# Rewriting the recurrent mixer of a two-block network: chunks of 64 tokens, one instruction block, key projection first

## The reference, cut to what matters

```python
def step(S, inp):                      # one token, state S per head: 64 x 64
    sa = einsum('bhvk,bhk->bhv', S, -kk_t)
    S = S * w_t + sa[..., None] * kka_t + v_t[..., None] * k_t
    y = einsum('bhvk,bhk->bhv', S, r_t)

xx = shift(h) - h;  xs = h + xx * mu           # six mixes: r, k, v, w, a, g
r, k, v = xs[:3] @ w_rkv                       # three 1024 x 1024 projections
decay   = exp(-exp(-softplus(-(w0 + tanh(xw @ w_la) @ w_lb)) - 0.5))
a = sigmoid(a0 + (xa @ a_la) @ a_lb);  g = sigmoid(xg @ g_la) @ g_lb
kk = normalise_per_head(k * k_k);  k = k * (1 + (a - 1) * k_a)
y = scan(step, r, decay, k, v, kk, kk * a)     # over 256 tokens
y = (group_norm(y) + bonus(r, k, r_k, v)) * g;  out = y @ w_o
```

## Time and profile before

| what | value |
|---|---|
| median of 3 runs | 2202.36 us (2195.92 to 2205.94) |
| the profiled execution, its time | 2182.94 us |
| its span | 2181.2 us |
| PE busy | 1899.2 us, 87% of the span |
| DVE busy | 830.6 us, 38% |
| ACT, POOL busy | 508.2 us, 138.0 us |
| mean granted PE clock | 0.926 |
| DMA traffic | 554.34 MB, 254 GB/s over the span |

### The profile page before, as it was taken

How to read it: one execution, slowest core, us unless ns; L and a number is a source line. 1 busy time by engine, 2 the same in 40 slices (tenths; PEclk the granted TensorE clock), 3 DMA queues, 4 the chain that set the end, 5 groups by cost and what they waited for, 6 DMA issues and landing times. The chain is left out here.

```text
span 2181.2 us, 28996 instructions
## 1 busy us (share of the span) xinstructions
PE 1899.2 (87%) x11494; PEld 1193.7 (55%) x11494; DVE 830.6 (38%) x1543; ACT 508.2 (23%) x807; POOL 138.0 (6%) x127
## 2 busy tenths in 40 slices
PE   6888599989989888898888789889988966898997
PEld 5675333333333333333333379779977656867996
DVE  7852511111111111111111266565543565446554
ACT  4421211101111110111111055345421141004442
POOL 3301210000000000000000000000000060200000
PEclk9968699999999999999999989999999986579998
DMA  7020699999999999999997275284425002108440
GB/s 271 34 107 1 257 404 428 428 428 429 428 428 429 428 429 428 429 428 429 428 428 323 101 295 188 78 308 155 154 74 204 0 20 66 52 1 308 154 154 30
DMA packets 99120, 554.34 MB, mean 254 GB/s; under 512 B 17473, under 2 KB 20418, under 8 KB 73618
## 3 DMA queue, kind: packets, MB, share of 16 engines
q1 hardware_dynamic: 99058, 553.49, 62.4%
HBM read 551.37 MB, written 2.10 MB: 254 GB/s over the span
## 5 line engine op out<-in xcount | busy, mean ns | idle before, releaser
L1009 PE MATMUL banks<-ring,xsT 128*64 128x512 f32 x2048 | 458.7, 598 | 41.9 <-DMA ring<-in_w_up 40.9
L1009 PEld LDWEIGHTS banks<-ring,xsT 128*64 128x64 f32 x2048 | 143.2, 137 | 351.3 <-issue 266.0
L1108 DVE TENSOR_SCALAR glu<-banks 128x512 f32<-128x512 f32 x32 | 22.1, 692 | 663.8 <-PE banks L1016 663.8
L1045 PE MATMUL banks<-ring,hT 128*64 128x512 f32 x1024 | 230.2, 603 | 22.0 <-ACT hT L1064 22.0
L1045 PEld LDWEIGHTS banks<-ring,hT 128*64 128x64 f32 x1024 | 71.5, 138 | 158.6 <-issue 130.5
L1546 PE MATMUL banks<-f_xT_hi,f_w_hi 128*128 128x256 f32 x512 | 146.8, 287 | 7.2 <-ACTq L1590 7.2
L1546 PE MATMUL banks<-f_xT_lo,f_w_hi 128*128 128x256 f32 x512 | 146.6, 286 | 0.0
L1546 PE MATMUL banks<-f_xT_hi,f_w_lo 128*128 128x256 f32 x512 | 146.6, 286 | 0.0
L1060 ACT ACTIVATE sig<-glu 128x512 f32<-128x512 f32 x32 | 20.1, 630 | 478.4 <-DVE glu L1108 478.4
L1546 PEld LDWEIGHTS banks<-f_xT_hi,f_w_hi 128*128 128x128 f32 x512 | 100.1, 195 | 9.4 <-DVE f_w_lo L1625 7.6
L1546 PEld LDWEIGHTS banks<-f_xT_lo,f_w_hi 128*128 128x128 f32 x512 | 100.1, 195 | 1.8
(11 more groups left out here) (383 smaller groups left out, 2992.6 us busy)
## 6 DMA issues: line engine op xcount, KB each, us to landing
ring<-in_w_up SPq DMA_DIRECT2D x128, 2048.0 KB, 24.7
ring<-in_w_down SPq DMA_DIRECT2D x64, 2048.0 KB, 20.3
ring<-in_ffn_w SPq DMA_DIRECT2D x32, 2048.0 KB, 7.8
ring<-in_sgu_in SPq DMA_DIRECT2D x8, 2048.0 KB, 7.6
m_raw<-in_w_in SPq DMA_DIRECT2D x7, 2048.0 KB, 10.3
ring<-in_w_rkv SPq DMA_DIRECT2D x6, 2048.0 KB, 20.4
ring<-in_sgu_out SPq DMA_DIRECT2D x4, 2048.0 KB, 7.6
ring<-in_w_out SPq DMA_DIRECT2D x1, 4096.0 KB, 16.4
```

Source lines behind the costliest of these rows:

```text
L1009: ins = nc.tensor.matmul(c.banks[CAP * h:CAP * (h + 1), bank, :], xsT[:, k, :], up_slot[k // 2][:, o:o + BANK], start=k == 0, stop=False)
L1045: ins = nc.tensor.matmul(c.banks[CAP * h:CAP * (h + 1), DOWN, :], hT[:, at:at + CAP], down_slot[half][:, o:o + BANK], start=k == 0, stop=k ...
L1108: v.tensor_scalar(glu[:, :], c.banks[:, GLU, :], LIMIT, None, ALU.min).then_inc(glu_ready, 1)
```

## The change

The stage becomes one instruction block with chunks of 64 tokens (four chunks, two for each 128 tokens), while the systems that are solved stay 32 x 32 (SUB = 32). What it does, by engine:

- PE starts with the k projection's first bank, then the low-rank products with the other k banks behind them, the sum of kk squared, the first bank of r, the spread of the inverse root, the second bank of r, A·B, the last two banks of r, the v projection, then the other grams, transposes, bonus and G_AK·v. A·B and all grams are made only for the 64 x 64 diagonal blocks, in products with 64 rows and 64 columns of the array.
- The value weights are loaded into the memory of the key weights once these are read.
- The two late r banks and the product with kT are taken by DVE inside the solve (`query`).
- The inverse of a 64-token chunk is put together from its two 32 x 32 inverses and the block between them (`own`, `cross`, `add_cross`), applied at once to A and to G_AK·v; P is then transposed.
- The walk has four chunks, of which the first has no incoming state. The output's products are made for each chunk (64 rows, 64 columns).
- The group norm's square moves to ACT, one POOL product (a times the inverse decay) is new, and `head_rk` folds r_k into the bonus selector.

Core of the diff:

```diff
-CH = 32
+CH = 64
...
-        w_rkv_sb = [unit(4 * i, 4).rearrange("p (k n) -> p k n", k=KC) for i in range(3)]
+        w_k, w_r = (unit(i, 4).rearrange("p (k n) -> p k n", k=KC) for i in (0, 4))
+        w_v = w_k
...
+                sp.wait_ge(k_done, 4)
+                for half in range(2):
+                    load_half(w_v, 2, half, v_in)
+                sp.wait_ge(ab_taken, 4)
+                for j in range(P // SUB):
+                    s, t = slice(SUB * j, SUB * (j + 1)), slice(SUB * (j % 2), SUB * (j % 2 + 1))
+                    sp.dma_start(dram_a[j].rearrange("n s t -> s n t"),
+                                 ab[s, :, :, t].rearrange("s c h t -> s (c h) t")).then_inc(a_out, 16)
...
+                for r in range(2):
+                    pe.wait_ge(chained, 2 * r + 2)
+                    for tc in range(TC):
+                        for p in range(4 * r, 4 * r + 4):
+                            for j in range(J):
+                                for par in range(2):
+                                    ins = nc.tensor.matmul(c.banks[rows_of(j), BANKS_AB[2 * r + par], o:o + CH],
+                                                           bT[part(par), p, t], ar[part(par), p, 0, t], start=True,
+                                                           stop=True)
+                    ins.then_inc(ab_done, 1)
+                pe.wait_ge(r_in[1], 16)
+                to_features(w_r, MIX_R, BANKS_R[2], 2, r_done)
+                to_features(w_r, MIX_R, BANKS_R[3], 3, r_done)
...
+                def own(m):
...
+                    for i in range(4):
+                        for j in range(J):
+                            ins = nc.tensor.matmul(c.banks[rows_of(j), m % 4, i * P:(i + 1) * P],
+                                                   inv[rows_of(j), tc, 4 * hq + i, :], right[rows_of(j), tc, 4 * hq + i, :],
+                                                   start=i == 0, stop=False, skip_group_check=True)
+                def cross(m):
...
+                            ins = nc.tensor.matmul(c.banks[late(j), 4 + m % 4, i * P:(i + 1) * P],
+                                                   ab[early(j), tc, h, SUB:CH], pu[early(j), :, tc, at_head(h)],
+                                                   start=True, stop=True)
+                def add_cross(m):
...
+                            ins = nc.tensor.matmul(c.banks[late(j), m % 4, i * P:(i + 1) * P],
+                                                   inv[late(j), tc, 4 * hq + i, SUB:CH], crossed[late(j), m % 4, i, :],
+                                                   start=False, stop=True, skip_group_check=True)
...
+                for tc in range(TC):
+                    for m in range(4 * tc, 4 * tc + 4):
+                        own(m)
+                    for m in range(4 * tc, 4 * tc + 4):
+                        cross(m)
+                    for m in range(4 * tc, 4 * tc + 4):
+                        add_cross(m)
...
+                state_from_values(0)
+                state_from_sa(0)
+                pe.wait_ge(pt_taken, 4)
+                y_from_values(0)
+                y_from_values(1)
+                y_from_sa(0)
+                sa_from_state(1)
+                state_from_values(1)
+                state_from_sa(1)
+                y_from_sa(1).then_inc(y_inner, 1)
+                pe.wait_ge(y_inner, 1)
+                y_from_state(1).then_inc(y_done, 1)
+                y_from_values(2)
+                y_from_values(3)
+                sa_from_state(2)
+                state_from_values(2)
+                state_from_sa(2)
+                y_from_sa(2)
+                sa_from_state(3)
...
+                y_from_sa(3).then_inc(y_inner, 1)
+                pe.wait_ge(y_inner, 2)
+                y_from_state(2)
+                y_from_state(3).then_inc(y_done, 1)
...
+                for t in range(1, SUB):
...
+                    if t == 2:
+                        query(2)
+                    if t == 8:
+                        query(3)
+                        dve.wait_ge(q_ready, 4)
+                        vec.tensor_tensor(prod, ar[:, :, 1, :], kT, ALU.mult).then_inc(prod_ready, 1)
```

More of the change, by code:

```diff
@@ new lines, in second_rank @@
+                def second_rank(lo, bank, b):
+                    for i in range(2):
+                        f = 2 * b + i
+                        ins = nc.tensor.matmul(c.banks[:, bank, i * T:(i + 1) * T],
+                                               wa_lb[lo:lo + LORA, f * P:(f + 1) * P],
+                                               hid[lo:lo + LORA, 0, :], start=True, stop=True)
+                    ins.then_inc(lb_done, 1)
+                pe.wait_ge(lora_in, 64)
+                pe.wait_ge(mixed, 1)
@@ new lines, in _ @@
+                low_rank(w_la, MIX_W, c.banks[0:LORA, 4, 0:T]).then_inc(la_done, 1)
+                pe.wait_ge(mixed, 2)
+                low_rank(a_la, MIX_A, c.banks[LORA:P, 5, 0:T]).then_inc(la_done, 1)
+                pe.wait_ge(mixed, 3)
+                pe.wait_ge(k_in[0], 16)
+                to_features(w_k, MIX_K, BANKS_K[0], 0, k_done)
+                pe.wait_ge(hid_w, 1)
+                for b in range(4):
+                    second_rank(0, BANKS_W_LB[b], b)
+                pe.wait_ge(mixed, 4)
@@ new lines, in _ @@
+                pe.wait_ge(gate_in, 32)
+                low_rank(g_la, MIX_G, c.banks[:, 4, 0:T]).then_inc(g_la_done, 1)
+                pe.wait_ge(hid_a, 1)
+                for b in range(4):
+                    if b >= 2:
+                        pe.wait_ge(sig_taken, b - 1)
+                    second_rank(LORA, BANKS_A_LB[b], b)
+                pe.wait_ge(sig_taken, 3)
+                to_features(w_k, MIX_K, BANKS_K[1], 1, k_done)
+                pe.wait_ge(k_in[1], 16)
+                pe.wait_ge(sig_taken, 4)
@@ L1863, in _ @@
                 ins.then_inc(bonus_done, 1)
[L1865 to L1875 removed]
+                n += 1
+                pe.wait_ge(bonus_taken, 1)
@@ new lines, in y_from_state @@
+                def y_from_state(n):
+                    tc, j = divmod(n, J)
+                    for h in range(RH):
+                        ins = nc.tensor.matmul(
+                            c.banks[rows_of(j), Y_B[2 * tc + h % 2], (h // 2) * HD:(h // 2 + 1) * HD],
+                            ar[part(h), h // 2, 1, n * CH:(n + 1) * CH],
+                            states[part(h), n, (h // 2) * HD:(h // 2 + 1) * HD], start=False, stop=True,
+                            skip_group_check=True)
+                    return ins
@@ L1877, in _ @@
+                for tc in range(TC):
+                    project(tc)
             @block.scalar
@@ new lines, in _ @@
+                act.wait_ge(g_la_done, 1)
+                nc.scalar.activation(hid[:, 1, :], c.banks[:, 4, 0:T], ACT.Sigmoid).then_inc(hid_g, 1)
+                for b in range(4):
+                    act.wait_ge(lb_done, 4 + b + 1)
+                    opened(a, "a0", BANKS_A_LB[b], b, a_taken)
+                act.wait_ge(run_ready, 1)
+                nc.scalar.activation(ar[:, :, 1, :], run, ACT.Exp, scale=-DECAY).then_inc(w_incl_ready, 1)
+                act.wait_ge(w_incl_ready, 1)
+                nc.scalar.activation(w_inv, run, ACT.Exp, scale=DECAY).then_inc(w_inv_ready, 1)
@@ L1963, in _ @@
-                last.then_inc(prod_ready, 1)
+                mix(MIX_W)
+                mix(MIX_A)
+                dve.wait_ge(la_done, 1)
+                mix(MIX_K)
+                dve.wait_ge(la_done, 2)
+                vec.tensor_copy(hid[LORA:P, 0, :], c.banks[LORA:P, 5, 0:T]).then_inc(hid_a, 1)
+                mix(MIX_G)
+                mix(MIX_R)
+                mix(MIX_V)
+                dve.wait_ge(sig_taken, 4)
+                dve.wait_ge(keep_ready, 2)
+                vec.tensor_tensor_scan(flat(run), flat(keep), flat(sig), 0.0, ALU.mult, ALU.add).then_inc(run_ready, 1)
```

1035 lines of the change are left out of this document (514 added, 521 removed).

## The result

| what | before | changed |
|---|---|---|
| median, runs on one chip | 2201.13 us (4 runs, 2195.92 to 2205.94) | 2104.19 us (4 runs, 2099.78 to 2107.77) |
| ratio | | 0.9559, 95% interval 0.9530 to 0.9588 |
| the profiled execution | 2182.94 us | 2103.96 us |
| the mixer's stage | 347.5 us | 267.3 us |

What follows compares the result with a forecast made beforehand. Mixer stage bound by projections before A·B, the relay through DVE, the walk and the tail; -45 + 19 - 31 + 4 = -53 gives 2130 from the profiled execution, 2149 against the median; range 2115 to 2180.

Steps and rivals of the forecast that it cites:

- Parts 1 to 3: Relay and PE's arrival: solve starts at 1727, 49 us earlier, stays 48 us; `own` starts at 1787, 45 us earlier.
- Rival 4: Relay not started earlier because DVE is late or ACT holds an eviction back; 15 us late gives 2160; chance 0.12.
- rival 3: Quadrants don't overlap, so each small product pays for itself at low clock: +64, 2266 us; chance 0.05.
- Part 4: Solution (`own`, `cross`, `add_cross`, transposes, eviction): 33 us where P and U took 13.9, +19.
- rival 1: Cold and serial in places: grams, transposes and solution could run at low clock; -18, 2184 us; chance 0.17.
- Part 5: Walk: 20 groups of 16 products priced at the 1.2 GHz level, 56 us against 86.9, -31.
- rival 2: The clock stays up in the walk, with some 3 us in the solution: -83, 2119 us; chance 0.11.
- Part 6: Tail: PE waits 4 us for the first group norm, then 36.7 us as before, +4.

Runs made afterwards that it cites:

- the run with quadrant products: Changed kernel with 128 extra 64 x 64 products, alternating between two quadrants, ahead of the walk's third group, results unused: 2111.72 us.
- halved forms: Changed kernel with the walk's state-group products split into two with 32 stationary columns or 32 rows, as in the old walk, 144 products added: 2136.5 us.
- the pause: Changed kernel with PE kept waiting ahead of the walk's third group for seven idle ACT copies: 2130.78 us.
- The run of the old kernel with the long first step: Old kernel, no edit, run and profiled again: median 2186.21 us of 13 runs; the profiled execution took 2201.63 us.

## Why the prediction was right up to the walk, and wrong about the walk's clock and its base

**Parts 1 to 3, the relay and PE's arrival: right.** DVE starts at 1727.7 (1727 said), ends at 1774.8 (1775), `own` starts at 1787.4 (1787). Inside, errors cancelled: A·B took 2.1 us and not 3.9, the grams 6.6 (1758.2 to 1764.8) and not 12, but A·B began at 1714.7 and not at 1711.9, and G_AK·v waited 7.5 us for POOL's masks, which at 1.33 us each took 21.3 and not 17.5. PE didn't wait for `chained`: it is busy without a gap up to A·B, and the second r bank took 8.86 us where the first took 7.17, as it ran at 0.56 for 3.9 us behind the products with 16 rows. Beside the solve the old kernel's PE had 32 us of work and not 38, a sum that counted A·B itself. POOL's masks cost the old solve 7.5 us in the first execution, where 6 were put down. The run with A·B late gives the value of this part. Rival 4 didn't come true. Nor did rival 3: 0.033 us for a product of A·B, where it needed 0.21 on average.

**Part 4, the solution: right, mis-sized by 5.** +14.2 for +19. Of rival 1 only patches of low clock came (0.88 over the solution). `own` took 3.71 us for 32 products, 0.12 each, at the low end of the bounds, because the two chunks' quadrants overlap, as the run with quadrant products showed (0.06 for 64 columns, 0.11 without overlap).

**Part 5, the walk: the step that failed.** The prediction put it: "so I price the new walk there at the 1.2 GHz level throughout". It ran at 2.4 GHz for all but its last 3 us, and -31 became -56. The mistake was to take the 0.50 of 1877 to 1915 for a property of a walk, where the runs show that it was one of the old walk's products: halved forms alone bring it on, entering the old walk at full clock doesn't prevent it. The counter-evidence stood in the trace of before: P and U, 128 columns wide, ran at 0.90, and the old walk itself began at 1.00, in a stretch (1846 to 1848) that no row shows by itself. The clock's share of the miss is about 20 us: behind the pause, at the low clock, 46.7 us passed for the part that takes 28.5, and the first two groups would have taken some 3.8 instead of 2.0 (an estimate from the two groups of 1.9 in that run). The rest, 5 us or so, is sizes: at the low clock the whole would have been near 50.5 us, not 56, mostly since a `y_from_state` group takes 1.5 us at that clock and not 2.3, and PE waits 0.9 us, not 2.

This is rival 2, "the clock stays up in the walk", with -83 against -80.2 measured, and it had a chance of 0.11. The Trainium skill's rule that was weighed there (TensorE: Matmul & The Clock Gate, "Why this matters for your kernels"), continuous work brings full clock, gave the right end for this walk but isn't what the runs show in general: 45.70 of 47 us busy at 0.51, 49.05 of 50 at 0.50, 60.63 of 62 at 0.50.

**Part 6, the tail: right, +6.6 for +4.** PE waits 6.06 us for the first norm because its own walk was shorter than thought; the norm takes what it takes.

**The number it was set against: the second step that failed.** The prediction: "the difference is in nothing that this change touches". The sum was 2130 against the profiled execution, and 19.4 were added to meet the median. The run of the old kernel with the long first step is longer than the profiled execution by 18.7 us, and 13.0 of them are DVE held up by POOL's masks at the start of the solve. The change moves both: the masks now meet only the solve's end. So most of that difference was in what the change touches. Where the other 5.7 us come from, 3.3 of them ahead of the stage, stays open, and so does what the four long runs of the first chip looked like inside. The changed kernel's median and its profiled execution agree within 0.3 us. The miss of 45 us is thus 27 from the sum (25 in Part 5, 5 in Part 4, less 2.6 in the tail), 19.4 from here, less 1.3 outside the stage.

**The range.** Its low end was rival 2's time less 4 us, counted from the median. From the profiled execution rival 2 would have given 2100, and a low end of 2100 would have held the result.

## What to carry to other kernels

A low granted clock in the stretch of before is a fact about the products and waits that are there; if a change replaces the products, price the new ones at both levels, and give both a real chance. When a profiled execution and the median of the runs differ by more than the usual spread, look for two engines that hold each other up inside the part that is changed before calling the difference foreign. And what paid in this relay through another engine was to start it early: that alone was worth 35 of the 80 us, while the two orders of the work behind it that were run lie 2.6 us apart.

## What was not expected of the hardware

- DVE's two-input product waited 20.62 us for a row of back-to-back POOL products of a microsecond each, not only for one; in another execution of the same kernel the two took turns.
- Products with 32 rows, without any wait, took PE from a granted clock of 1.00 to 0.50, and behind products with 16 rows it fell in both unedited kernels; products of 64 x 64 in the same place held 1.00 for 24 us, and load-bound ones of 128 x 64 for 9 us, yet at 0.50 the 64 x 64 ones of the walk didn't bring it back in 46 us. The 128-column products of the solution and the transposes did: 0.50 in 1799 to 1801 and 1.00 in 1802 to 1811, 0.59 in 1812 to 1816 and 1.00 in 1816 to 1840.
- A stop of 0.51 us in the walk cost 1.0 us; one of 1.15 cost 14 us.

Open is how forms and stops weigh together: the solution has stops of 0.36 us and products of 32 x 32, it falls to 0.50 for some microseconds twice (about 1798.4 to 1801.5 and 1812 to 1815) and is at 1.00 between (1802 to 1811, through 32 x 32 products with 128 columns moving), and no run takes out the one or the other.
